# First loads of attention issued in the block before it, scan products moved between levels, gate products paired on opposite array halves

## The chip, the core and the metric

One NeuronCore of a Trainium2 chip runs the whole program. The metric is the device time of one execution in microseconds (us), given as the median of several runs. Names used below: PE is TensorE's matmul, PEld its weight load, DVE is VectorE, ACT is ScalarE, POOL is GpSimd, SP is SyncE, which here only issues transfers. L785 is line 785 of the kernel before.

## What is computed

Two trunk layers run over 128 context tokens and 512 latent tokens, all float32. Layer 0 projects the tokens once (21 blocks of 128 columns) and feeds two head groups: attention with a sink logit, and a bidirectional RWKV-7 time mixer. Layer 1 is a convolution module. Both layers end in an expert retrieval (PEER). The parts of the reference that the change touches are the mixer's decay and learning rate, and its scan:

```python
logw = -jax.nn.softplus(-(w0[idx] + jnp.tanh(wl) @ w2[idx])) - 0.5
decay = jnp.exp(-jnp.exp(logw))
a = jax.nn.sigmoid(a0[idx] + al @ a2[idx])
...
s = (s * w_t[:, :, None, :]
     - jnp.einsum('bhvk,bhk->bhv', s, kh_t)[..., None] * ka_t[:, :, None, :]
     + v_t[..., None] * kt_t[:, :, None, :])
```

and the modulation `jax.nn.silu(cond) @ w + b`, whose weights (mod_w, 48 pieces of 1 MB) are streamed beside other work.

## The kernel before, in words

All TensorE work lies in blocks, one after the other; between two blocks all engines meet at a barrier, and each engine runs its own instructions in the order written.

**The first block** (phase_front, to 267.9 us) normalises the tokens, makes the first modulation rows and projects the 21 column blocks. The projection goes by 42 ticks: in each, TensorE multiplies half a column block (L330, L331), and a side program (`operands`, run by `Side`) puts the mixer's small products between ticks. For step n of 8 (four groups of 128 columns, two directions) `gates(n)` (L335) multiplies the decay weights w2 into bank pair A and the learning-rate weights a2 into bank pair B. Both contract over 64 rows: rows 0 to 63 of the array for direction 0, rows 64 to 127 for direction 1. Each is two matmuls of 320 columns (`mm640`, L205 to L208). ScalarE turns A and B into `ld` and `a` (L482), VectorE builds the scan's operands (`multiply`, L607), and `bonus` (L365, L624) makes a head sum; the last bonus is read by VectorE at L626, four ticks before the end. SP's part of this block only issues loads of column blocks.

**The attention block** (phase_attention, 267.9 to 394.2 us): SP issues the cached keys, the rotation matrix, the cosine and sine table (rope), the mask and others, then modulation steps 0 to 4 into a ring of five 1 MB places (L733 to L738), then small rows. A later step m is issued when step m - 5 has been multiplied (L742 to L744). TensorE turns values and keys, rotates queries and keys (L771), multiplies modulation steps 0 to 3 (L819), and then goes through 20 pairs of heads and query tiles; in each it does the scores of the next pair (L781, L785), two transposes, the weighted values and two modulation steps. 40 steps are streamed in all. When step 38 is done, POOL loads the scan's masks and states.

**The scan block** (phase_scan, 394.2 to about 676 us) goes through 10 chunks of 64 tokens for two directions g. A chunk has five levels of a triangular inverse: `level` multiplies (into M, copied by ScalarE at L1172), `refine` multiplies by it, VectorE merges the result under a mask (L1249), and the next `level` of the same g needs that merge. Then come `solve`, `finish` and the state update (L1279, L1281). Four products of the next chunk (turned_keys, values, first_products, second_products) are prepared meanwhile. `beside` alternates matmuls of its arguments, which use different quadrants of the array. Before the change the order is:

```python
for l in range(LEVELS):
    for g in range(G):
        if l and i + 1 < N:
            beside(level(g, i, l), steps[l - 1](g, i + 1))
        elif l:
            beside(level(g, i, l))
    for g in range(G):
        refine(g, i, l)
    if l == 0:
        for g in range(G):
            beside(weigh_state(g, i))
```

**The trunk** (phase_trunk, from 676 us) does the rest: output projection, layer 1 and both expert retrievals, with 1280 indirect loads. The change doesn't touch it.

Of the kernel before, what the change touches and what calls it, by code (L numbers as in the profile page):

```python
# [173 lines left out]
def mod_lanes(r):  # L174
    return slice(32 * r, 32 * r + 2)
# [38 lines left out]
def phase_front(K, ring, small, normed, dump, u, q1, q2, k1, k2, pc, mixT, low):  # L214
# [17 lines left out]
    with ExitStack() as mem:  # L232
# [25 lines left out]
        with nc.Block() as block:  # L258
            @block.sync
            def _(sp):  # L260
# [35 lines left out]
            def _(pe):  # L296
# [37 lines left out]

                def gates(n):  # L335
                    cols, rows = slice(n // 2 * P, (n // 2 + 1) * P), slice(64 * (n % 2), 64 * (n % 2) + 64)
# [4 lines left out]
                    elif n % 2 == 0 or n == 1:  # L341
                        pe.wait_ge(S["kh_done"], n // 2 + 1)
                    else:
# [21 lines left out]
                def bonus(cc):  # L365
                    if cc == NCC - 1:
                        pe.wait_ge(S["bonus_read"], cc)
                    else:
                        pe.wait_ge(S["a_done"], 2 * cc + 4)
# [8 lines left out]
                def operands():  # L378
# [6 lines left out]
                    for n in range(N):  # L385
                        cc, d = n // 2, n % 2
                        yield step_tick(n)
                        if n + 1 < N:
                            gates(n + 1)
# [35 lines left out]
            def _(act):  # L425
# [56 lines left out]
                def gates(n):  # L482
# [4 lines left out]
                    nc.scalar.activation(ld[:, p, :], ps[:, A, SQ:EQ], ACT.Sigmoid, bias=vcol("ab_w0", 4 * d + cc)).then_inc(S["sig_done"], 1)  # L487
                    act.wait_ge(S["az_done"], n + 1)
# [14 lines left out]
                def operands():  # L503
# [14 lines left out]
                    rates(0)  # L518
                    for n in range(N):
# [142 lines left out]

class ScanParts:
# [5 lines left out]
    def __init__(self, K, u, at):  # L669
# [4 lines left out]
        self.staging = [at(f"levels{n}", [P, self.LM], K.base + 140800 + 8192 * n) for n in range(2)]  # L674
        self.raw = at("raw", [P, G, NCC, CH], K.base + 140800 + 8192 * 2)
# [18 lines left out]
def phase_attention(K, qT, kT, vT, mixT, scan_parts):  # L694
# [3 lines left out]
    with ExitStack() as mem:  # L698
        sb = lambda n, s, d=F32: mem.enter_context(nc.sbuf_tensor("at_" + n, s, d))
        in_x = lambda n, s, at: nc.alloc_sbuf_tensor_at("at_" + n, s, F32, offset=K.x_at + at)  # L700
        ring = sb("ring", [P, MOD_PLACES, 4 * 512])
        mask = sb("mask", [P, 7 * P])
        mod, normg, rope = in_x("mod", [P, MOD_LATER, 512], 0), in_x("normg", [P, 2, 512], 10240), in_x("rope", [P, 2, T_LAT], 14336)
        perm, kctx, vctx, kcT = (in_x(n, [P, P], 18432 + 512 * a) for a, n in enumerate(("perm", "kctx", "vctx", "kcT")))
        kvtok = sb("kvtok", [P, NT + 1, P])
        sink = scan_parts.spare
        s, pT = sb("s", [P, 4, 4 * P]), sb("pT", [P, 2, 4 * P])
        rot = s[:, 2:4, :]
        st = sb("st", [P, 4, 6])
        assert nc.sbuf_base <= K.base + HEADS_AT  # L710
        m_in = [K.sem(f"at_m_in{a}") for a in range(MOD_PLACES)]
# [5 lines left out]
        keys_in, rope_in, rest_in, kv_turned, kv_copied, kv_out = (K.sem("at_" + n) for n in ("keys_in", "rope_in", "rest_in", "kv_turned", "kv_copied", "kv_out"))  # L717
# [6 lines left out]
        with nc.Block() as block:  # L724
            @block.sync
            def _(sp):
                sp.dma_start(kctx[:], io["cache_k"][0, 0].rearrange("t g e -> t (g e)")).then_inc(keys_in, 16)
                sp.dma_start(perm[:], K.const["ropeperm"]).then_inc(keys_in, 16)
# [1756 lines left out]
```

## Time and profile before

| | |
|---|---|
| time, median of 3 runs | 4194.36 us (4193.69 to 4196.37) |
| the profiled execution's own time | 4194.05 us |
| its span in the trace | 4192.3 us |
| first block, to the barrier | 0 to 267.9 us |
| attention block | 267.9 to 394.2 us |
| scan block | 394.2 to about 676 us |
| trunk | the remaining 3516 us |
| busy, share of the span | PE 73%, DVE 65%, ACT 38%, POOL 36% |
| chain that ended last, by engine | DMA 43%, PE 21%, DVE 9%, ACT 5%, issue 4% |

The chain of the page is an average over the whole program, and the trunk, at 84% of the span, fills it. The changed code runs in the first 676 us, so the stages there are read one by one. Times in the trace are counted from the start of the span.

### The profile page before, as it was taken

The page shows a single profiled execution, that of the slowest core. Times are in us where ns is not written, and L with a number is a line of the kernel's source. Part 1 is how long each engine was busy: PE and PEld are TensorE (multiplying, and loading weights), DVE is VectorE, ACT ScalarE, POOL GpSimd, SP SyncE. Part 2 cuts the span into 40 slices and gives each one's busy share as a digit, 9 for nine tenths or more (in the row PEclk, how much of TensorE's full clock was granted, in tenths as well). Part 3 has the DMA queues.
Part 4 walks back from the last instruction along what each step waited for, and adds up shares of the span by engine and source line. Part 5 has one row for each costly group of instructions (what it writes and reads, how often), then busy time and mean ns, then how long its engine had stood idle before and what let it go on. Part 6 is the DMA issues. An engine that isn't in the chain of part 4 may idle for free.

```text
span 4192.3 us, 67991 instructions
## 1 busy us (share of the span) xinstructions
PE 3054.5 (73%) x25020; PEld 1460.5 (35%) x25020; DVE 2745.0 (65%) x6901; ACT 1596.6 (38%) x4953; POOL 1489.7 (36%) x1307
## 2 busy tenths in 40 slices
PE   8988878887875555588866768887685666666555
PEld 5645776433331111134421434442241231132111
DVE  2646445776666676667876566786756787756764
ACT  3524322343332332345533334553333463322332
POOL 0000000443444444434533444454434454443433
PEclk9999999989997777799987988998798898888877
DMA  4147002999999999999999999999999999999998
GB/s 170 41 184 288 7 4 113 409 420 420 419 412 419 412 419 421 417 412 402 420 396 363 419 420 419 416 420 411 395 419 421 421 419 417 415 419 417 413 421 334
DMA packets 228426, 1507.71 MB, mean 360 GB/s; under 512 B 31086, under 2 KB 32073, under 8 KB 57601
## 3 DMA queue, kind: packets, MB, share of 16 engines
q0 software_dynamic: 185216, 1343.99, 77.7%
q1 hardware_dynamic: 42440, 159.26, 9.7%
q8 instruction: 202, 3.31, 0.3%
q14 instruction: 126, 1.03, 0.1%
q10 hardware_dynamic: 442, 0.12, 0.0%
HBM read 1500.17 MB, written 3.10 MB: 359 GB/s over the span
## 4 chain that ended last, share of the span: by engine, by line
DMA 43%; PE 21%; DVE 9%; ACT 5%; issue 4%; POOL 2%; SPq 0%; PEldq 0%; ACTq 0%; POOLq 0%; DVEq 0%
DMA t_ring<-in_peer_uv,t_eidx 41%; PE t_ps L2419 10%; DVE t_ring L1747 6%; PE t_ps L2297 2%; POOL t_ring L1609 2%; PE t_ps L2316 1%; ACT t_dg L1938 1%; ACT t_wgt L1932 1%; DMA t_wq<-in_cv_w_pw 1%; PE t_ps L2345 1%; PE t_ps L2161 1%; PE t_ps L2253 1%; PE t_ps L2375 1%; ACT t_wgt L1927 1%; PE t_ps L2257 1%
## 5 line engine op out<-in xcount | busy, mean ns | idle before, releaser
L1609 POOL DMA_INDIRECT t_ring<-in_peer_uv,t_eidx x1280 | 1477.0, 1154 | 2302.2 <-PE t_ps L2422 1799.0
L2419 PE MATMUL t_ps<-t_ring,t_dg 64*64 64x512 f32 x2560 | 1556.2, 739 | 991.4 <-ACT t_dg L1938 934.4
L1747 DVE SCALAR_TENSOR_TENSOR t_ring<-t_ring,t_hring 128x1024 f32<-128x1024 f32 x1024 | 1255.8, 1227 | 772.9 <-DMA t_ring<-in_peer_uv,t_eidx 723.3
L2422 PE MATMUL t_ps<-t_ring,t_dg 64*64 64x512 f32 x2560 | 1572.7, 746 | 0.0
L2421 PE MATMUL t_ps<-t_ring,t_dg 64*64 64x512 f32 x2560 | 1572.5, 746 | 0.0
L2420 PE MATMUL t_ps<-t_ring,t_dg 64*64 64x512 f32 x2560 | 1572.2, 746 | 0.0
L2419 PEld LDWEIGHTS t_ps<-t_ring,t_dg 64*64 64x64 f32 x2560 | 344.3, 155 | 1981.2 <-issue 1954.8
L1927 ACT ACTIVATE t_wgt<-t_dots 128x2 f32<-128x2 f32 x640 | 130.3, 204 | 1916.3 <-DVE t_ring L1747 1874.9
L1938 ACT ACTIVATE t_dg<-t_eye,t_wgt 128x64 f32<-128x64 f32 x1280 | 376.0, 340 | 1.3 <-ACT t_wgt L1932 1.1
L2422 PEld LDWEIGHTS t_ps<-t_ring,t_dg 64*64 64x64 f32 x2560 | 345.0, 156 | 0.0
L2421 PEld LDWEIGHTS t_ps<-t_ring,t_dg 64*64 64x64 f32 x2560 | 344.9, 156 | 0.0
L2420 PEld LDWEIGHTS t_ps<-t_ring,t_dg 64*64 64x64 f32 x2560 | 344.8, 156 | 0.0
L1932 ACT ACTIVATE t_wgt<-t_wgt,t_gate 128x1 f32<-128x1 f32 x1280 | 307.3, 287 | 28.5 <-DVE t_gate L1722 2.8
L1747 DVE SCALAR_TENSOR_TENSOR t_ring<-t_ring,t_h_latent 128x1024 f32<-128x1024 f32 x128 | 157.2, 1228 | 116.1 <-DMA t_ring<-in_peer_uv,t_eidx 102.8
L1747 DVE SCALAR_TENSOR_TENSOR t_ring<-t_ring,t_h_context 128x1024 f32<-128x1024 f32 x128 | 156.9, 1226 | 97.6 <-DMA t_ring<-in_peer_uv,t_eidx 94.7
L2316 PE MATMUL t_ps<-t_glu,t_diag 128*128 128x256 f32 (+1 forms) x930 | 188.8, 356 | 0.0
L2316 PEld LDWEIGHTS t_ps<-t_glu,t_diag 128*128 128x128 f32 x930 | 153.5, 194 | 68.0 <-ACT t_diag L1994 39.6
L1927 ACT ACT_TABLE_LOAD x113 | 145.0, 1283 | 17.1 <-DVE t_ring L1747 15.2
L2375 PE MATMUL t_ps<-t_pair,t_wq 128*128 128x256 f32 (+1 forms) x768 | 151.3, 351 | 0.0
L1994 ACT ACTIVATE t_diag<-ident,vec 128x128 f32<-128x128 f32 x465 | 143.3, 387 | 0.9 <-PE t_ps L2316 0.6
L2375 PEld LDWEIGHTS t_ps<-t_pair,t_wq 128*128 128x128 f32 x768 | 129.1, 198 | 15.2 <-issue 3.2
L684 POOL DMA_DIRECT2D ev_u<-const_scanmask x1 | 0.6, 557 | 367.9 <-PE at_mps L819 367.9
(385 smaller groups left out, 4499.2 us busy)
## 6 DMA issues: line engine op xcount, KB each, us to landing
at_ring<-in_mod_w SPq DMA_DIRECT2D x40, 1024.0 KB, 10.9
t_wq<-in_peer_w_q SPq DMA_DIRECT2D x62, 512.0 KB
t_ring<-in_peer_uv,t_eidx POOLq DMA_INDIRECT x1280
t_wg<-in_cv_w_pw SPq DMA_DIRECT2D x32, 512.0 KB
t_wq<-in_cv_w_pw SPq DMA_DIRECT2D x24, 512.0 KB
fr_wring<-in_ab_w_in SPq DMA_DIRECT2D x21, 512.0 KB, 3.5
ev_mod_ring<-in_mod_w SPq DMA_DIRECT2D x8, 1024.0 KB, 18.5
t_wg<-in_peer_w_q SPq DMA_DIRECT2D x16, 512.0 KB
```

The lines of the kernel that those rows point to most:

```text
L1609: pool.indirect_dma_start(ring[:, place[n], :], None, table, bass.IndirectOffsetOnAxis(ap=eidx[:, s % 2, r:r + 1], axis=0)).then_inc(row_i ...
L1747: V.scalar_tensor_tensor(ring[:, place[n], 0:D], ring[:, place[n], 0:D], 1.0, h_of(j), ALU.mult, ALU.mult, accum_out=dots[:, j % 2, r:r + ...
L1927: nc.scalar.activation(wgt[:, r:r + 2], dots[:, j % 2, r:r + 2], ACT.Gelu).then_inc(S["gelu_done"], 1)
L1932: nc.scalar.activation(wgt[:, r + b:r + b + 1], wgt[:, r + b:r + b + 1], ACT.Copy, scale=gate[:, j % 2, r + b:r + b + 1]).then_inc(S["wgt_ ...
L1938: nc.scalar.activation(dg[:, n % DIAGS, :], eye[:], ACT.Copy, scale=wgt[:, r + b:r + b + 1]).then_inc(S["diag_set"], 1)
L1994: nc.scalar.activation(diag[:, n % BATCH, :], ident[:], ACT.Copy, scale=K.vec[:, col:col + 1]).then_inc(S["diag_ready"], 1)
L2316: nc.tensor.matmul(tiles_of(banks[:, 4 + b % 2, :], p), diag[:, n % BATCH, :], windows(p, b, w), start=(w == 0), stop=(w == CONVW - 1)).th ...
L2375: last = nc.tensor.matmul(tiles_of(banks[:, 6 + b % 2, :], p), wq[:, n % 2, k, :], both[:, k, 0:E, :], start=(k == 0), stop=(k == KD - 1))
L2419: nc.tensor.matmul(straight[low], diagonal[low], row[low, 0:512], **ends)
L2420: nc.tensor.matmul(straight[high], diagonal[high], row[high, 0:512], **ends)
L2421: nc.tensor.matmul(crossed[high], diagonal[low], row[low, 512:D], **ends)
L2422: nc.tensor.matmul(crossed[low], diagonal[high], row[high, 512:D], **ends).then_inc(S["used"], 1)
```

## The change

Three things are done, and one follows from them.

1. **Gate products.** `gates(n)` now makes the decay product of step n and the learning-rate product of step n - 1, in four alternating matmuls (first 320 columns of both, then last 320 of both). Step n and step n - 1 have opposite directions, so the two products lie on opposite 64-row halves of the array. Step 0 has the decay product alone, and a new `gates(8)` has the last learning-rate product alone. ScalarE's `gates` is split, and `learning(n)` follows `gates(n + 1)`.
2. **First loads of attention.** After VectorE's last bonus read, SP issues keys, rotation matrix, rope table and modulation steps 0 to 3 in the first block. For that the five ring places are moved (two lie in the x area, two over the front's small weights, the fifth where the transposed tokens lie until the end of the projection, so step 4 is still issued in the attention block).
3. **Scan order.** turned_keys is put beside weigh_state instead of beside level 1. For levels 2 to 4 the product of g = 0 runs alone before `level(0, i, l)`, and that of g = 1 stays beside `level(1, i, l)`.
4. Tiles of the scan and of attention move in memory; VectorE waits for the mask copies before it clears the state, which now lies where the masks were staged.

```diff
@@ phase_front, sync @@
+                sp.wait_ge(S["bonus_read"], NCC)
+                attention_parts.load_ahead(sp, K)
@@ phase_front, tensor @@
                 def gates(n):
+                    halves = ((SQ, 512, 0, SPLIT), (512, EQ, SPLIT, T))
...
-                    mm640(nc, ps, A, w2[rows, cols], u[rows, 12, :]).then_inc(S["z_done"], 1)
-                    if n in (4, 6):
+                    if n >= 4 and n % 2 == 0:
                         pe.wait_ge(S["bonus_read"], n // 2 - 1)
-                    elif n:
-                        pe.wait_ge(S["a_done"], n)
-                    mm640(nc, ps, B, a2[rows, cols], u[rows, 13, :]).then_inc(S["az_done"], 1)
+                    elif n >= 2:
+                        pe.wait_ge(S["a_done"], n - 1)
+                    for lo, hi, first, last in halves:
+                        if n < N:
+                            cols, rows = gate_of(n)
+                            z = nc.tensor.matmul(ps[:, A, lo:hi], w2[rows, cols], u[rows, 12, first:last], start=True, stop=True)
...
+                        if n:
+                            cols, rows = gate_of(n - 1)
+                            az = nc.tensor.matmul(ps[:, B, lo:hi], a2[rows, cols], u[rows, 13, first:last], start=True, stop=True)
...
@@ phase_front, scalar @@
-                            rates(n + 1)
+                        learning(n)
+                        rates(n)
                         exponents(n)
@@ AttentionParts (new) @@
+    def load_ahead(self, sp, K):
+        sp.dma_start(self.kctx[:], ...).then_inc(self.keys_in, 16)
+        sp.dma_start(self.perm[:], ...).then_inc(self.keys_in, 16)
+        sp.dma_start(self.rope[:], ...).then_inc(self.rope_in, 16)
+        for m in range(MOD_EARLY):
+            self.load_step(sp, K, m)
@@ phase_attention, sync @@
-                for m in range(MOD_PLACES):
-                    load_step(m)
+                for m in range(MOD_EARLY, MOD_PLACES):
+                    parts.load_step(sp, K, m)
@@ phase_scan, tensor @@
+                    ahead = i + 1 < N
+                    for g in range(G):
+                        refine(g, i, 0)
+                    for g in range(G):
+                        if ahead:
+                            beside(weigh_state(g, i), turned_keys(g, i + 1))
+                        else:
+                            beside(weigh_state(g, i))
+                    for l in range(1, LEVELS):
+                        if ahead and l > 1:
+                            beside(steps[l - 1](0, i + 1))
+                        beside(level(0, i, l))
+                        if ahead and l > 1:
+                            beside(level(1, i, l), steps[l - 1](1, i + 1))
+                        else:
+                            beside(level(1, i, l))
                         for g in range(G):
                             refine(g, i, l)
```

## Rows read from the trace of the kernel before

**Rows 1.** the page: the span; TensorE's granted clock in 40 slices

```profile
span 4192.3 us, 67991 instructions
...
PEclk9999999989997777799987988998798898888877
```

**Rows 2.** stages: length, busy PE, PEld, DVE, ACT, POOL; PEclk, DMA, GB/s

```profile
60.00:267.00 207.00, 205.08 (x733) 136.65 (x731) 103.86 (x152) 88.62 (x125) 0.00 (x0) 0.98 0.13 44
267.00:394.00 127.00, 101.86 (x841) 43.49 (x841) 86.31 (x281) 52.94 (x169) 5.19 (x9) 0.93 0.89 355
394.00:676.00 282.00, 234.73 (x9344) 218.61 (x9344) 129.64 (x265) 83.32 (x242) 0.00 (x0) 0.99 0.05 15
676.00:4192.00 3516.00, 2472.98 (x13888) 1036.49 (x13888) 2409.57 (x6168) 1353.37 (x4384) 1476.97 (x1280) 0.86 0.99 408
```

**Rows 3.** timeline, TensorE: first and last matmul of one step's gates

```profile
157.50 0.80 PE L207 MATMUL fr_ps<-ev_u,fr_w 64*128 64x320 f32 x2
...
159.22 0.70 PE L208 MATMUL fr_ps<-ev_u,fr_a 64*128 64x320 f32 x2
```

**Rows 4.** the line view of L785: durations, then matmuls in a moment

```profile
L785 PE MATMUL at_ps_s<-ev_u x4: 482/484/485, 330.9 to 331.2; 64*128 64x384 f32 x4
...
331.19:331.23 0.04, 0.04 (x4) 0.00 (x0) 1.00 0.51 205
```

**Rows 5.** timeline, around the last bonus product (start us, length, engine)

```profile
239.06 0.88 DVE L649 SCALAR_TENSOR_TENSOR ev_kt<-ev_ktsum,fr_rkh,ev_u 128x640 f32<-128x640 f32 x1
...
252.74 0.70 PE L207 MATMUL fr_ps<-ev_kt,fr_hsum 128*128 128x320 f32 x2
...
254.01 0.82 DVE L626 TENSOR_TENSOR ev_u<-fr_ps,ev_u 128x640 f32<-128x640 f32 x1 [14.07 <-PE fr_ps L208]
```

**Rows 6.** timeline, first loads and rotations of the attention block

```profile
267.90 0.33 SPq L727 DMA_DIRECT2D at_kctx<-in_cache_k  x1
...
273.19 0.69 DVE L850 TENSOR_TENSOR at_s<-at_ps_s,at_rope 128x512 f32<-128x512 f32 x1 [18.36 <-DMA at_rope<-const_rope]
...
278.67 0.50 PEld L771 LDWEIGHTS at_ps_s<-ev_u,at_perm 128*128 128x128 f32 x2 [1.53 <-DVEq L853]
...
282.62 28.15 SPq L734 DMA_DIRECT2D at_ring<-in_mod_w  x12
...
284.93 1.04 PE L819 MATMUL at_mps<-at_ring,csil 128*2 128x512 f32 x8 [1.03 <-DMA at_ring<-in_mod_w]
```

**Rows 7.** stretches of the attention block, columns as in rows 2

```profile
270.00:275.00 5.00, 2.45 (x6) 1.04 (x7) 1.66 (x3) 0.54 (x2) 0.00 (x0) 1.00 0.82 250
275.00:279.50 4.50, 3.59 (x5) 1.01 (x4) 4.21 (x8) 0.00 (x0) 0.00 (x0) 0.65 0.96 406
...
300.00:330.00 30.00, 25.29 (x228) 9.70 (x220) 21.89 (x74) 11.50 (x42) 0.00 (x0) 1.00 1.01 419
```

**Rows 8.** the modulation ring: its issues, who waited for its transfers

```profile
at_ring<-in_mod_w SPq DMA_DIRECT2D x40, 1024.0 KB, 10.9
...
  PEld at_mps L819: 22.9, 17
```

**Rows 9.** eight chunks of the scan, and the slowest, columns as in rows 2

```profile
433.85:654.20 220.35, 180.58 (x7458) 167.47 (x7447) 101.45 (x209) 66.56 (x195) 0.00 (x0) 1.00 0.03 6
570.82:601.49 30.67, 22.68 (x946) 20.96 (x950) 12.63 (x27) 8.24 (x25) 0.00 (x0) 1.00 0.02 4
```

**Rows 10.** TensorE's waits in the scan: us, times, longest

```profile
PE sc_ps L1014 <- issue: 30.7, 40, 1.8
PE sc_ps L1014 <- DVE ev_u L1249: 10.5, 24, 0.6
```

**Rows 11.** the scan between two idle times; the instruction queue's packets

```profile
552.13 0.27 PE L1014 MATMUL sc_ps<-ev_u 64*64 64x64 f32 x2 [0.73 <-issue]
...
552.13:556.03 3.90, 2.66 (x127) 2.52 (x128) 1.00 0.02 4
...
q8 instruction: 74, 1.21, 1.7%
```

More of the change, by code:

```diff
@@ L211, with phase_front @@
 ORDER = [D_AIN // P + j for j in (12, 13, 4, 5, 6, 7, 0, 14, 8, 1, 9, 2, 10, 3, 11)] + [0, 1, 2, 4, 5, 3]
-def phase_front(K, ring, small, normed, dump, u, q1, q2, k1, k2, pc, mixT, low):
+def phase_front(K, ring, small, normed, dump, u, q1, q2, k1, k2, pc, mixT, low, attention_parts):
     nc, io, x, ident = K.nc, K.io, K.x, K.ident
@@ L333, in project, with gate_of @@
                         last.then_inc(S["block_done"], 1)
+                def gate_of(n):
+                    return slice(n // 2 * P, (n // 2 + 1) * P), slice(64 * (n % 2), 64 * (n % 2) + 64)
                 def gates(n):
[L336 removed]
+                    halves = ((SQ, 512, 0, SPLIT), (512, EQ, SPLIT, T))
                     if n == 0:
@@ L487, in gates, with learning @@
                     nc.scalar.activation(ld[:, p, :], ps[:, A, SQ:EQ], ACT.Sigmoid, bias=vcol("ab_w0", 4 * d + cc)).then_inc(S["sig_done"], 1)
+                def learning(n):
+                    cc, d, p = n // 2, n % 2, n % 2
                     act.wait_ge(S["az_done"], n + 1)
@@ L673, in __init__ @@
         self.spare = u[:, 14, 0:HEADS]
-        self.staging = [at(f"levels{n}", [P, self.LM], K.base + 140800 + 8192 * n) for n in range(2)]
-        self.raw = at("raw", [P, G, NCC, CH], K.base + 140800 + 8192 * 2)
+        self.staging = [at(f"levels{n}", [P, self.LM], K.base + 177664 + 3072 * n) for n in range(2)]
+        self.raw = at("raw", [P, G, NCC, CH], K.base + 175616)
         K.heads = at("heads", [P, 2, P], K.base + HEADS_AT)
@@ L699, in phase_attention @@
         sb = lambda n, s, d=F32: mem.enter_context(nc.sbuf_tensor("at_" + n, s, d))
[L700 to L705, printed above, removed]
-        sink = scan_parts.spare
-        s, pT = sb("s", [P, 4, 4 * P]), sb("pT", [P, 2, 4 * P])
+        places, rope, perm, kctx = parts.places, parts.rope, parts.perm, parts.kctx
+        m_in, keys_in, rope_in = parts.m_in, parts.keys_in, parts.rope_in
+        sink = scan_parts.spare
+        sb("place4", [P, 4 * 512])
+        normg, mod = sb("normg", [P, 2, 512]), sb("mod", [P, MOD_LATER, 512])
+        mask, kvtok = sb("mask", [P, 7 * P]), sb("kvtok", [P, NT + 1, P])
+        vctx, kcT = sb("vctx", [P, P]), sb("kcT", [P, P])
+        pT, st = sb("pT", [P, 2, 4 * P]), sb("st", [P, 4, 6])
+        assert nc.sbuf_base <= K.base + 175616
+        sb("between", [P, (K.base + 192000 - nc.sbuf_base) // 4])
+        s = sb("s", [P, 4, 4 * P])
         rot = s[:, 2:4, :]
-        st = sb("st", [P, 4, 6])
-        assert nc.sbuf_base <= K.base + HEADS_AT
-        m_in = [K.sem(f"at_m_in{a}") for a in range(MOD_PLACES)]
+        assert nc.sbuf_base <= K.base + 200192
         mps = mem.enter_context(nc.psum_tensor("at_mps", [P, 2, 512], F32))
@@ L818, in modulation @@
                     for r in range(4):
-                        last = nc.tensor.matmul(mps[mod_lanes(r), g % 2, :], K.csil[:, k, :], ring[:, m % MOD_PLACES, r * 512:(r + 1) * 512],
+                        last = nc.tensor.matmul(mps[mod_lanes(r), g % 2, :], K.csil[:, k, :], places[m % MOD_PLACES][:, r * 512:(r + 1) * 512],
                                                 start=(k == 0), stop=(k == KD - 1))
@@ L1130, in _ @@
                 for i in range(N):
-                    for l in range(LEVELS):
-                        for g in range(G):
-                            if l and i + 1 < N:
-                                beside(level(g, i, l), steps[l - 1](g, i + 1))
-                            elif l:
-                                beside(level(g, i, l))
+                    ahead = i + 1 < N
[14 more added lines that the diff above has]
+                            beside(level(1, i, l))
                         for g in range(G):
                             refine(g, i, l)
-                        if l == 0:
-                            for g in range(G):
-                                beside(weigh_state(g, i))
                     for g in range(G):
```

53 lines of the change are left out of this document (34 added, 19 removed).

## The prediction

> **What bounds the kernel now.** I read the page first, then stretches by stage, then timelines and waits. The page gives a span of 4192.3 us [rows 1]. The stage view [rows 2] splits it, and each stage has its own limit. From 60 to 267 us PE is busy for 205.1 of 207 us: the projection is limited by TensorE, and whatever leaves its queue leaves the time. From 267 to 394 us the transfers are at 355 GB/s, in the middle at 419 GB/s with a share of 1.01 [rows 7]: attention is limited by the stream of modulation weights, and weight loads of L819 wait 22.9 us for them [rows 8]. From 394 to 676 us no engine is full: PE 234.7 of 282 us. The rest is two kinds of waits: 10.5 us for VectorE's masked merge (24 times), and 30.7 us, 40 times, of "issue", in which TensorE waited for nothing that the profile shows [rows 10]. The trunk keeps the DMA engines at 0.99 for 3516 us; nothing in it is touched and it starts at a barrier, so it should move as a whole by what the first three stages give.
>
> The sum is made against the profiled execution's own 4194.05 us, which is 1.75 us more than its span. The median of the runs is 4194.36, 0.3 us higher.
>
> **Part 1, gate products.** In a step four matmuls of 64 rows and 320 columns start at 157.50 to 159.22 us, in even steps: the last begins 1.72 us after the first, so one takes about 0.54 us after the extra 0.1 us of the first [rows 3]. Four are 2.15 us a step, eight steps 17.2 us, all in TensorE's full queue. Do opposite halves overlap? The scores of the two head groups lie on opposite halves in separate banks, as the new pairs will: at 331.2 us four of their records, of 0.48 us each, run at once, and all four start between 330.9 and 331.2 [rows 4]. Two after two would need twice that. So an interleaved pair should take the time of one. New sum: step 0 alone 1.07, seven paired visits 7 x 1.07, the last learning-rate product 1.07, in all 9.7 us. **Gain 7.5 us.** Bounds: no overlap 0, full overlap 7.5; I take 7.5, since the row is the same form.
>
> What moves with it: `a` of step n comes one gate visit later, still in the same step, and VectorE makes the running sums of step n + 1 before it wants it. The tight place is the end. Before, VectorE finished the last bonus operand at 239.06 + 0.88 us, and TensorE took it up at 252.74 - 0.13, a margin of over 12 us [rows 5]. The last learning rate now comes at tick 35, one tick ahead of the last output gate: about 238.7 us by the old clock, ready for VectorE near 241, where the old `multiply` of step 7 began at 233.2. The bonus operand then ends near 239.9 + 7.8 = 247.7, and about 5 us of margin are left. If they were gone, TensorE would stand there and the loads behind it too. ScalarE has the same instructions in another order, and costs nothing while TensorE is full.
>
> **Part 2, loads ahead.** VectorE reads the last bonus at 254.01 + 0.82 us [rows 5]; the block ends 13 us later, when SP issues the keys at 267.90 [rows 6]. Both move with part 1. SP has nothing queued behind its new wait except the barrier, where TensorE arrives 12 us later. The seven issues take about 0.45 us each (3.2 us) and leave the attention block's SP queue; mask, sink, values and step 4 go 3 us sooner. Nothing else moves data there, so 4.85 MB (four steps of 1.05, rope 0.52, two of 0.07) land in about 11.6 us at 419 GB/s, near the barrier.
>
> Times now are counted with the barrier at its old place. Rope was waited for until 273.19 us [rows 6]; now VectorE starts when the first rotation is made, near 269.7. The chain is 3.5 us earlier, its last rotation at 278.67 - 3.5 = 275.2. Step 0 follows, near 275.8. PE's granted clock is 0.65 from 275 to 279.5 us, so partly at the lower level of 1.2 GHz [rows 7], after rotations with idle time between them, which the new order keeps. A step takes 0.95 us at the full clock [rows 6] and twice that at the lower. So step 0 is done near 277.7, step 5 is issued, and its data moves from about 279.5. Before that the ring has a dry spell: only mask, values and step 4 are asked for. This is the price of moving four loads and not the fifth.
>
> Compare bytes at 279.5 us. New: 4.85 ahead + 0.46 + 0.07 + 1.05 and small rows = 6.6 MB. Old: 0.2 + 5 x 0.250 + 4.5 x 0.406 = 3.3 MB [rows 7]. Later both stream at 0.419 MB/us with the same ring, so the new one is 3.3 / 0.419 = **8 us ahead**, and SP's tail, POOL's loads and the barrier with it. Bounds: if pairs, not transfers, set the pace, only the rope's 3.5 us; if the dry spell costs nothing, four steps of 2.5 us, 10 us. The narrow early pairs have slack to catch up with the stream, so I take 8.
>
> **Part 3, scan order.** A product of four head pairs takes about 0.47 us, a merged one of eight about 1.05. Putting turned_keys beside weigh_state saves about 0.94 us of a chunk, of which 0.2 comes back as a wait for the copy of M. In levels 2 to 4 a lone product of 0.5 to 0.9 us fills a wait of 10.5 / 24 = 0.44 us and makes level 0's half shorter: some 0.2 us each. By this walk a chunk gains 1.3 us, nine chunks 12 us.
>
> But the issue idles have a pattern. From one at 552.13 to the next at 556.03 us are 127 matmuls and 128 weight loads, 3.90 us [rows 11]; I found 22 more such neighbours, 126 to 128 matmuls apart, 3.4 to 5.0 us, mean 3.84. Over the scan the instruction queue moved 1.21 MB in 74 packets [rows 11], 16 KB each, one per 3.8 us. So TensorE waits for its own instructions, one packet per 128 matmuls. Eight chunks took 220.35 us with 7458 matmuls: 27.5 us a chunk, 7.3 packets, 3.78 us a packet [rows 9]. That is already the interval between starved neighbours. The reordering removes no instruction, so what it saves turns into a longer issue idle. Bounds: the full 12 us, or a loss if every packet took 3.84 us: 0.06 x 65 = 4 us. I take **2 us**, near the fetch-limited end, as most chunks are there.
> The Trainium skill, "Runtime: NRT & Kernel Launch", section "Instruction fetch mechanics", says that crossing a 16 KiB boundary costs one DMA tail-bump and is mostly hidden. By that rule the walk's 12 us would come. The trace disagrees so far, with 0.77 us of idle per starved boundary.
>
> The wait for the mask copies costs nothing: VectorE's queue holds both copies ahead of it, and TensorE is at its first products then.
>
> **Sum:** 7.5 + 8 + 2 = 17.5 us. 4194.05 - 17.5 + 0.3 = 4176.9; I say 4177.
>
> **Rivals.**
> - *Fetch is not the limit.* Against: the even spacing. For: 74 packets stand against 40 issue idles, so close to half of the boundaries show none. Then 12 in place of 2: 4167. Chance 0.15.
> - *Attention turns to the pairs' pace.* For: in the wide pairs PE is nearly full. Then 3.5 in place of 8: 4181. Chance 0.14.
> - *The pairing doesn't happen*: the array takes both halves in turn, 0 in place of 7.5: 4184. Against: rows 4. Chance 0.06.
> - *Slower.* Instruction fetch gets worse where TensorE is denser and waits for nothing else. The slowest chunk took 30.67 us [rows 9], 3.1 more than the mean. If all nine became like it, 28 us more: 4194.4 - 15.5 + 28 = 4207. A packet interval of 4.0 us over nine chunks (0.22 x 66 = 14.5 us) eats the other gains, and one of 4.2 gives the 28. Chance 0.04.
> - *Most of it is given back*, by the margin at the end of the front and by starved packets together: 4188 to 4194. Chance 0.1.
>
> **Numbers.** The forecast has 0.51. 0.2% is 8.4 us, about what a measurement of this kernel can tell from no change, so faster means below 4186. Forecast, the first two rivals and most of the third lie there: 0.84. The fifth and a piece of the third give 0.12 for no change, the slower rival 0.04. The range reaches from just below the first rival, 4163, to 4188, which leaves out the slower rival and part of the fifth.
>
> **What would show it.** Right: the block's barrier 7.5 us earlier, seven gate visits with all four matmuls within some 1.3 us; SP's loads near 247 us; rope no longer waited for; a stretch of low transfer rate between the barrier and step 5; last ring issue some 15 us earlier; scan chunks of about 27.3 us with fewer waits on L1249 and more issue idle. Wrong: chunks near 26 us without issue idles, or above 28; weight loads of a pair starting one after the other; no wait of L819 for transfers in the early pairs.

## The result

The changed kernel takes 4170.92 us (median of 5 runs, 4169.54 to 4176.78), the kernel before 4194.36 beside it: ratio 0.9947, 95% interval 0.9936 to 0.9957. Its profiled execution took 4169.54 us. The page of the changed kernel:

```profile
span 4167.8 us, 67998 instructions
...
PE 3026.0 (73%) x25020; PEld 1449.8 (35%) x25020; DVE 2744.5 (66%) x6901; ACT 1600.3 (38%) x4955; POOL 1518.4 (36%) x1307
...
PEclk9999999999997877799977979998897897888787
```

Its stages, with their borders at the barriers and at the first matmul of the trunk; columns as in [rows 2]:

```profile
60.00:259.49 199.49, 195.72 (x730) 130.19 (x728) 103.75 (x152) 90.48 (x126) 0.00 (x0) 0.99 0.20 68
259.49:375.43 115.94, 96.95 (x841) 44.32 (x842) 86.29 (x281) 52.20 (x168) 5.18 (x9) 0.96 0.87 349
375.43:662.00 286.57, 233.10 (x9344) 217.39 (x9344) 129.39 (x265) 83.14 (x242) 0.00 (x0) 0.99 0.05 14
662.00:4167.80 3505.80, 2459.99 (x13888) 1031.76 (x13888) 2409.22 (x6167) 1355.31 (x4384) 1505.68 (x1280) 0.86 1.00 409
```

To set beside them, the same borders of before are 267.90, 394.20 and 677.92 us. So the first block is 8.4 us shorter, attention 10.4 us shorter (115.9 for 126.3), the scan **2.9 us longer** (286.6 for 283.7) and the trunk, which nobody touched, 8.6 us shorter (3505.8 for 3514.4). In all 24.5 us of span, 15.9 of them in the three stages that the change touches.

**Gates.** The timeline of TensorE over one step (start us, length, engine), to set beside [rows 3]:

```profile
151.94 0.53 PE L357 MATMUL fr_ps<-ev_u,fr_w 64*128 64x320 f32 x1
151.95 0.53 PE L362 MATMUL fr_ps<-ev_u,fr_a 64*128 64x320 f32 x1
...
152.86 0.43 PE L357 MATMUL fr_ps<-ev_u,fr_w 64*128 64x320 f32 x1
152.86 0.43 PE L362 MATMUL fr_ps<-ev_u,fr_a 64*128 64x320 f32 x1
153.22 0.81 PE L332 MATMUL fr_ps<-fr_hT,fr_wring 128*128 128x320 f32 x2
```

Each decay product (L357) and the learning-rate product of the other half (L362) start together. From the first to the projection's next matmul are 1.28 us; before, 157.50 to 159.84, it was 2.34.

**End of the front and loads ahead.** The timeline around the last bonus, and of the attention block's first operations:

```profile
238.35 0.89 DVE L666 SCALAR_TENSOR_TENSOR ev_kt<-ev_ktsum,fr_rkh,ev_u 128x640 f32<-128x640 f32 x1
...
244.31 0.70 PE L207 MATMUL fr_ps<-ev_kt,fr_hsum 128*128 128x320 f32 x2
...
245.59 0.82 DVE L643 TENSOR_TENSOR ev_u<-fr_ps,ev_u 128x640 f32<-128x640 f32 x1 [6.36 <-PE fr_ps L208]
246.44 0.33 SPq L695 DMA_DIRECT2D ev_kctx<-in_cache_k  x1
...
247.76 1.90 SPq L692 DMA_DIRECT2D ev_mod_place<-in_mod_w  x4
...
261.45 0.69 DVE L884 TENSOR_TENSOR at_s<-at_ps_s,ev_rope 128x512 f32<-128x512 f32 x1 [15.03 <-PE at_ps_s L805]
...
267.98 3.61 PE L853 MATMUL at_mps<-ev_mod_place,csil 128*2 128x512 f32 x32
...
269.08 2.90 SPq L692 DMA_DIRECT2D ev_mod_place<-in_mod_w  x4
```

VectorE finished the last bonus operand at 239.24 us (238.35 + 0.89) and TensorE took it up at 244.31 - 0.13, so the margin was 4.9 us and held. Rope is no longer waited for: VectorE's first rotation comes 2.0 us after the barrier and not 5.3, and what it waited for is PE. Step 5 is issued 9.6 us after the barrier. Transfers between, and the clock (columns as in [rows 2]):

```profile
264.00:266.00 2.00, 1.11 (x2) 0.30 (x2) 1.85 (x4) 0.00 (x0) 0.00 (x0) 1.00 1.03 402
266.00:268.00 2.00, 1.09 (x7) 0.32 (x9) 1.85 (x4) 0.00 (x0) 0.00 (x0) 1.00 0.31 86
268.00:270.00 2.00, 2.00 (x21) 0.50 (x24) 1.85 (x4) 0.00 (x0) 0.00 (x0) 1.00 0.13 33
```

This is the dry spell. The last issue of the ring is at 352.63 us, 18.7 us earlier than before (371.33).

**Scan.** The eight chunks that answer to [rows 9]:

```profile
416.77:638.18 221.41, 178.87 (x7455) 166.69 (x7447) 100.91 (x209) 66.37 (x195) 0.00 (x0) 1.00 0.03 6
```

TensorE's waits over these eight chunks, as in [rows 10]:

```profile
PE sc_ps L1050 <- issue: 36.6, 41, 2.0
PE sc_ps L1088 <- issue: 3.2, 5, 1.0
```

And the packets of the instruction queue in them (packets, MB, share):

```profile
q8 instruction: 59, 0.97, 1.9%
```

The 8.9 us for the masked merge that the same eight chunks of before had are gone, and the issue idles grew from 27.8 to 39.8 us. The eight chunks take 221.4 us for 220.4, with 59 packets in both kernels.

### The profile page after: what moved, and what is told of

The parts are those of the page before. It is cut to its first block, busy times and chain, and to the rows that moved or that the text cites. A ratio compares the mean times of both kernels' runs of the same rounds, so it can differ in the third digit from the quotient of the medians.

```text
span 4167.8 us, 67998 instructions
## 1 busy us (share of the span) xinstructions
PE 3026.0 (73%) x25020; PEld 1449.8 (35%) x25020; DVE 2744.5 (66%) x6901; ACT 1600.3 (38%) x4955; POOL 1518.4 (36%) x1307
## 4 chain that ended last, share of the span: by engine, by line
DMA 46%; PE 19%; DVE 8%; ACT 5%; issue 3%; POOL 3%; SPq 0%; POOLq 0%; PEldq 0%; ACTq 0%; DVEq 0%
DMA t_ring<-in_peer_uv,t_eidx 44%; PE t_ps L2463 9%; DVE t_ring L1791 5%; POOL t_ring L1653 3%; PE t_ps L2341 2%; PE t_ps L2360 2%; ACT t_dg L1982 1%; DMA t_wq<-in_cv_w_pw 1%; ACT t_wgt L1976 1%; PE t_ps L2389 1%; PE t_ps L2419 1%; ACT t_wgt L1971 1%; PE t_ps L2205 1%; PE t_ps L2464 1%; ACT L1971 0%
## 5 line engine op out<-in xcount | busy, mean ns | idle before, releaser
L1653 POOL DMA_INDIRECT t_ring<-in_peer_uv,t_eidx x1280 | 1505.7, 1176 | 2266.7 <-PE t_ps L2466 1751.9
L1982 ACT ACTIVATE t_dg<-t_eye,t_wgt 128x64 f32<-128x64 f32 x1280 | 376.6, 340 | 1.0 <-ACT t_wgt L1976 0.2
```

The lines of the kernel that those rows point to most:

```text
L1653: pool.indirect_dma_start(ring[:, place[n], :], None, table, bass.IndirectOffsetOnAxis(ap=eidx[:, s % 2, r:r + 1], axis=0)).then_inc(row_i ...
L1982: nc.scalar.activation(dg[:, n % DIAGS, :], eye[:], ACT.Copy, scale=wgt[:, r + b:r + b + 1]).then_inc(S["diag_set"], 1)
```

## Experiments

In the table "barrier" is the end of the first block, "scan" goes from its first matmul to the trunk's first, "eight chunks" between the last state updates of the first and the ninth chunk, "trunk" from there to the end of the last instruction with a tile, all of one profile each; the medians are of all runs, and one in brackets is a single run. The kernel before was timed again beside each group: 4191.01 us beside gates alone, loads alone, scan order alone and gates and loads; 4193.41 beside again, same half, delay and five ahead; 4187.81 beside six ahead, fewer instructions and the two halves. These three medians of one kernel differ by 5.6 us.

| kernel | barrier | attention | scan | eight chunks | trunk starts | trunk | median | ratio, 95% |
|---|---|---|---|---|---|---|---|---|
| before | 267.9 | 126.3 | 283.7 | 220.4 | 677.9 | 3511.3 | 4194.36 | |
| changed | 259.5 | 115.9 | 286.6 | 221.4 | 662.0 | 3502.7 | 4170.92 | 0.9936 to 0.9957 |
| changed, again | 259.5 | 115.8 | 287.5 | 221.0 | 662.8 | 3501.7 | 4169.20 | 0.9927 to 0.9954 |
| gates alone | 260.1 | 126.5 | 284.8 | 221.5 | 671.4 | 3503.7 | 4179.56 | 0.9962 to 0.9983 |
| loads alone | 267.9 | 117.6 | 284.8 | 220.2 | 670.2 | 3505.2 | 4179.73 | 0.9958 to 0.9983 |
| scan order alone | 267.9 | 126.3 | 285.5 | 219.8 | 679.8 | 3509.5 | 4190.99 | 0.9991 to 1.0009 |
| gates and loads | 260.5 | 115.5 | 283.4 | 219.6 | 659.3 | 3504.5 | 4170.46 | 0.9941 to 0.9968 |
| same half | 268.1 | 115.6 | 285.8 | 221.3 | 669.6 | 3504.9 | (4179.32) | |
| delay | 260.2 | 115.5 | 301.7 | 218.8 | 677.4 | 3504.8 | 4192.00 | 0.9990 to 1.0009 |
| five ahead | 260.1 | 116.5 | 282.9 | 218.7 | 659.5 | 3502.7 | 4169.31 | 0.9930 to 0.9957 |
| six ahead | 259.3 | 114.2 | 282.0 | 217.6 | 655.4 | 3509.0 | 4168.28 | 0.9936 to 0.9963 |
| fewer instructions | 259.8 | 115.7 | 275.4 | 211.0 | 650.9 | 3500.8 | (4156.54) | |
| half, new order | 259.3 | 118.0 | 315.0 | 246.7 | 692.3 | 3506.0 | (4203.19) | |
| half, old order | 259.2 | 118.2 | 338.3 | 268.9 | 715.7 | 3508.2 | (4228.73) | |

**Gates alone.** The kernel before with the change of `gates`, `bonus` and `rates` only:

```diff
-                    mm640(nc, ps, A, w2[rows, cols], u[rows, 12, :]).then_inc(S["z_done"], 1)
...
+                    for lo, hi, first, last in halves:
...
+                            z = nc.tensor.matmul(ps[:, A, lo:hi], w2[rows, cols], u[rows, 12, first:last], start=True, stop=True)
...
+                            az = nc.tensor.matmul(ps[:, B, lo:hi], a2[rows, cols], u[rows, 13, first:last], start=True, stop=True)
```

> The kernel before with the gate products alone changed. My theory: four matmuls of opposite halves take the time of two, so the first block's barrier comes 7.5 to 8.5 us earlier (267.9 to about 259.8 us) and attention and scan keep their lengths, 126.3 and 283.7 us; in all about 4186. Rival A, the pairing is worth nothing and the earlier barrier of the changed kernel came from less time at the lower clock: barrier within 3 us of 267.9. Of the trunk: if its 8.6 us shorter time in the changed kernel was caused by the new attention or scan, it stays near 3514 us here; if it comes from where the trunk falls in time or varies from run to run, it may be anywhere from 3503 to 3516.

The barrier came at 260.1, 7.8 us earlier, and attention and scan kept their lengths within 1.1 us. The theory stands, the rival falls. The median is 4179.56 beside 4191.01, so 11.5 us lower where 8 were expected: here too the trunk is short (3503.7), with the attention and the scan of before, so its shorter time needs neither of their changes.

**Same half.** One line of the changed kernel:

```diff
-                            cols, rows = gate_of(n - 1)
+                            cols, rows = gate_of(n - 1)[0], gate_of(n)[1]
```

> The changed kernel in which the learning-rate product of a visit takes the rows of the decay product beside it, so both stand on the same half of the array (the learning rates come out with the other direction's weights and are wrong). Same matmuls in the same order. Theory of the opposite halves: each of seven visits takes four times 0.54 us and not two, so the barrier of the first block comes 7 x 1.07 = 7.5 us later, at 267.0. Rival, the interleaving or the order gives the gain and not the halves: barrier at 259.5.

The timeline of a visit shows the two kinds taking turns, 0.54 us a product (two records of the trace, 0.27 us each), and the barrier's first issue comes where it was before:

```profile
155.78 0.80 PE L357 MATMUL fr_ps<-ev_u,fr_w 64*128 64x320 f32 x2
...
156.42 0.70 PE L362 MATMUL fr_ps<-ev_u,fr_a 64*128 64x320 f32 x2
...
156.96 0.70 PE L357 MATMUL fr_ps<-ev_u,fr_w 64*128 64x320 f32 x2
...
157.49 0.70 PE L362 MATMUL fr_ps<-ev_u,fr_a 64*128 64x320 f32 x2
...
268.13 0.33 SPq L767 DMA_DIRECT2D at_mask<-const_amask  x1
```

Same matmuls in the same order, 8.6 us later than in the changed kernel: the opposite halves are the whole gain. It is 1.1 us more than expected, because the second visit took 3.5 us in this profile: the granted clock was 0.50 from 124.4 to 131.2 us. The other six took 2.35 us each.

**Loads alone.** The kernel before with `AttentionParts`, its places and these lines:

```diff
+                sp.wait_ge(S["bonus_read"], NCC)
+                attention_parts.load_ahead(sp, K)
```

> The kernel before with the loads ahead alone (and the new places in memory). My theory: first block unchanged (barrier near 267.9), attention 116 to 118 us in place of 126.3, scan unchanged at about 283.7; in all about 4185. Rival: the gain in attention needed the denser first block of the paired gates, which left the clock at its higher level for step 0; then attention takes 118 to 120 us. As with the first kernel the trunk tells whether its 8.6 us belong to a part of the change.

Attention took 117.6 us, within the theory's numbers, but 1.7 us longer than in the changed kernel. Here TensorE's clock fell in the rotations, and steps 0 and 1 ran at the lower level; the four steps took 4.66 us, where the changed kernel's took 3.61:

```profile
272.00:274.00 2.00, 1.09 (x3) 0.30 (x2) 1.85 (x4) 0.00 (x0) 0.00 (x0) 1.00 0.67 260
274.00:276.00 2.00, 1.09 (x3) 0.30 (x2) 1.85 (x5) 0.00 (x0) 0.00 (x0) 0.93 0.79 294
276.00:278.00 2.00, 2.00 (x10) 0.25 (x12) 1.85 (x4) 0.00 (x0) 0.00 (x0) 0.50 0.17 44
278.00:280.00 2.00, 2.00 (x17) 0.34 (x12) 1.85 (x4) 0.00 (x0) 0.00 (x0) 0.72 0.14 30
```

Step 5 was issued 11.0 us after the barrier in place of 9.6. In the changed kernel the same rotations and steps have a granted clock of 1.00 (the windows above). So the loads are worth 8.7 us in this profile, and 10.4 with the clock still high.

The rival says that the paired gates kept the clock up. Two other kernels speak against it. *Half of the products* is the changed kernel up to the scan, paired gates and all, and in both of its profiles the clock fell in the rotations just so, with 118.0 and 118.2 us of attention:

```profile
267.00:269.00 2.00, 2.00 (x6) 0.15 (x9) 1.85 (x4) 0.00 (x0) 0.00 (x0) 0.57 0.24 77
269.00:271.00 2.00, 2.00 (x16) 0.39 (x12) 1.85 (x4) 0.00 (x0) 0.00 (x0) 0.57 0.05 14
```

*Same half*, whose gates gain nothing, kept the clock, issued step 5 at 9.6 us after its barrier and took 115.6 us:

```profile
276.00:278.00 2.00, 2.00 (x18) 0.40 (x20) 1.85 (x4) 0.00 (x0) 0.00 (x0) 1.00 0.28 81
```

So the clock in the rotations can go either way with the same code up to there, and it is worth some 2 us of attention. What decides it isn't shown. The median of loads alone is 4179.73 beside 4191.01, 11.3 us lower where 9 were expected.

**Scan order alone**, and **gates and loads** with the old order, were each the before or the changed kernel with this part in the other form:

```diff
-                            if l and i + 1 < N:
-                                beside(level(g, i, l), steps[l - 1](g, i + 1))
...
+                            beside(weigh_state(g, i), turned_keys(g, i + 1))
...
+                        if ahead and l > 1:
+                            beside(steps[l - 1](0, i + 1))
```

> The kernel before with the scan's order alone changed. Theory of the instruction fetch: the waits for the merge vanish and the time stays, since not one instruction is removed: scan 283.7 to 287 us against 283.7, time 0 to 3 us above before, packets of the instruction queue 3.76 to 3.80 us apart. Rival, the scan of the changed kernel is held back by something the other parts brought (the moved staging places, the memory): then the scan gets shorter here, by up to 12 us.

> The changed kernel with the scan's old order, that is the gates and the loads alone. Theory: as fast as the changed kernel or up to 3 us faster, so 4168 to 4172; scan 283.7 us in place of 286.6. Rival, the new order helps the time as a whole (by the state in which it leaves the trunk): 4176 to 4180, with a trunk of 3514 us.

The order alone lengthened the scan by 1.8 us and changed the median by nothing; without it the changed kernel's scan is 3.2 us shorter. Over all profiles the old order takes 282.0 to 284.8 us (six, mean 283.6), the new one 285.5 to 287.5 (four, mean 286.4). These two ranges don't touch. But with the delay kernel as a fifth of the new order they do, up to the last state update of the ninth chunk: 257.8 to 261.0 us in the old order, 259.2 to 263.4 in the new one. By the means 1.0 us more lies ahead of the first chunk's last state update (41.2 for 40.1 us) and 0.8 in the eight chunks (220.5 for 219.6). So the new order probably costs 1 to 3 us; the profiles of one order differ by as much among themselves, and the medians don't show it. Eight chunks of the scan order alone, then TensorE's waits in them:

```profile
435.66:655.45 219.79, 179.00 (x7458) 167.02 (x7448) 100.83 (x208) 66.34 (x194) 0.00 (x0) 1.00 0.03 6
```

```profile
PE sc_ps L1014 <- issue: 37.2, 45, 2.0
PE sc_ps L1014 <- DVE ev_u L1254: 1.2, 7, 0.2
```

The queue moved 59 packets in them. Again the waits went and issue idle took their place.

**Fewer instructions.** The changed kernel, `heads` of the chunk's output with one half of each pair after the first chunk:

```diff
-                            for e in range(2):
+                            for e in range(both):
...
-                    yield from heads(region(g, 5), None, (at(state(i), g), chunk(q2, g, i)), (v, at(BD[:, i % 2, :, 1], g)), (at(U, g), at(ET[:, i % 2], g)))
+                    yield from heads(region(g, 5), None, (at(state(i), g), chunk(q2, g, i)), (v, at(BD[:, i % 2, :, 1], g)), (at(U, g), at(ET[:, i % 2], g)), both=2 if i == 0 else 1)
```

> The changed kernel; from the second chunk on, the second half of each pair of products of the chunk's output (24 of some 932 matmuls of a chunk, and their 24 weight loads) is left out, so half of the heads have no output of the scan there. A pair on opposite halves runs side by side, so TensorE saves no time by it. Theory of the fetch: 48 instructions less are 0.19 of a 16 KB packet, at 3.78 us 0.7 us a chunk and 5.7 us over eight; scan 281 to 282 us against 287, packets still 3.75 to 3.80 us apart. Rival, the engine's own work or the chain of merges sets the chunk: scan 286 to 287.5.

Its eight chunks, then the packets in them:

```profile
417.82:628.77 210.95, 177.90 (x7088) 167.11 (x7083) 99.18 (x208) 66.42 (x194) 0.00 (x0) 1.00 0.03 6
```

```profile
q8 instruction: 56, 0.92, 1.8%
```

**Half of the products**, in the new and in the old order: the same `both` in nearly all products of the scan. What is left of each pair lies on one half of the array's rows, rows 0 to 63 for most products and rows 64 to 127 for some (`refine`, `solve`).

> The changed kernel; from the second chunk on nearly all products of the scan are made for the first half of each pair alone (its other half of the heads is wrong), so a chunk has about half its instructions and each pair's time is that of its first matmul. Theory of the fetch: 3.7 packets a chunk need 14 us and are no limit; a chunk falls from 27.6 us to what the walk of products and copies gives, 22 to 24.5 us, the issue idles are gone, and waits for merges and copies are back. Rival, packets don't matter: 27 us as now, or, if the two halves did not overlap after all, far below 20.

> The same half of the products with the scan's old order (and gates and loads as changed). Theory: without the fetch limit the new order is worth what the walk gave it, so a chunk takes 1.3 us more here than in the new order, 10 us over eight chunks. Rival, the walk itself was wrong and the new order is worth nothing even then: within 0.3 us a chunk.

The eight chunks and 200 us out of their middle, in the new and then in the old order:

```profile
414.26:661.00 246.74, 245.31 (x3755) 239.34 (x3751) 102.94 (x208) 66.47 (x194) 0.00 (x0) 0.53 0.02 3
...
461.00:661.00 200.00, 199.33 (x2927) 195.19 (x2927) 79.94 (x162) 51.87 (x151) 0.00 (x0) 0.50 0.01 2
```

```profile
415.46:684.37 268.91, 262.03 (x3755) 252.48 (x3751) 103.13 (x209) 66.99 (x195) 0.00 (x0) 0.54 0.01 3
...
461.00:661.00 200.00, 197.13 (x2660) 190.26 (x2657) 72.34 (x145) 48.23 (x139) 0.00 (x0) 0.50 0.01 2
```

Their packets in the eight chunks, new order:

```profile
q8 instruction: 30, 0.49, 0.8%
```

and 31 in the old one. Half of the work took **longer**, 30.8 and 33.6 us a chunk. None of the numbers that I gave came, since the clock fell: in the new order the granted clock is 0.50 from 435 us to the end of the scan, with TensorE busy 99% of the time; in the old one it was 1.00 for a while around 450 us and is 0.50 from 461 us on. But two things can be read. A packet lasts 8.2 and 8.7 us here, and in the new order the list of matmul waits is empty from 440 us on: with half of the packets the fetch is no limit. And where it is none, the new order is the faster one: in the same 200 us at the same clock it makes 2927 matmuls and the old one 2660, 10% more. In the last six of the eight chunks, all at 0.50, that is 31.6 us a chunk for 35.0. The direction is the walk's, from one profile of each kernel. What the order is worth with few instructions at the full clock was not measured.

**Five and six steps ahead**, both with the old scan order. The fifth step goes to a place that is dead after the last bonus; the sixth is asked for at the barrier, without a wait, into the place that step 4 had. From the kernel of six ahead:

```diff
+        self.first4 = at("mod_place4_first", [P, 4 * 512], K.base)
...
-        for m in range(MOD_EARLY):
+        for m in range(MOD_EARLY + 1):
...
-                for m in range(MOD_EARLY, MOD_PLACES):
-                    parts.load_step(sp, K, m)
+                parts.load_step(sp, K, MOD_EARLY + 1)
```

> Gates and loads of the changed kernel, the scan's old order, and the fifth step of weights loaded ahead as well, into the place of en and kt, which nothing reads after the last bonus. Theory: the dry spell of the ring (0.1 to 0.3 of the transfer rate for 5 us) gets longer by what the fifth step used of it, but the stream is one step of 1.05 MB ahead: last issue of the ring 2 to 2.5 us earlier than 353.19, scan starts near 373.7, about 2 us below the kernel of gates and loads: 4168. Rival, the pairs' pace is the limit by then and nothing is gained: scan starts at 376.

> Gates and loads of the changed kernel, old scan order, step 4 loaded ahead into the place of en and kt, and step 5 asked for at the barrier without a wait into the place that step 4 had, so that there is something to move in the dry spell. Theory: the fifth step alone gave nothing because it landed in the dry spell anyway; a sixth fills it, and the stream from then on is one step, 1.05 MB / 0.42 = 2.5 us, ahead: scan starts at 373 to 374 in place of 376, in all 4167. Rival, TensorE's pairs set the pace by now (its waits for transfers fell from 12.9 to 6.1 us with the fifth step ahead and the scan began no sooner): 376, and 4169 to 4170 as now.

Five ahead missed: the scan began at 376.6, and the last issue came 0.6 us later. As I read it, it could not have gained, because in the kernel of gates and loads step 4 had landed in the dry spell anyway; the next thing that moves, step 5, was issued at 269.72 and 270.05 us, 9.6 us after the barrier in both. That attention is 1.0 us longer says little: in that profile the granted clock was 0.50 for 10.2 us of the block's first 40, in that of gates and loads for 3.4. Six ahead began the scan at 373.5 us, in the range expected, with 261 GB/s over five us where the changed kernel has 118 (265 to 270 us):

```profile
264.00:269.00 5.00, 3.40 (x16) 0.92 (x20) 4.56 (x8) 0.00 (x0) 0.00 (x0) 1.00 0.69 261
```

That is 1.3 us of attention, half of the 2.5 us expected; 1.2 us of the earlier start are the barrier's. In the median it doesn't show (4168.28 beside a before of 4187.81, the changed kernel's 4169.20 beside 4193.41), so no version here is measurably faster than the changed kernel, though this one's trunk starts 6.6 us earlier.

**The trunk.** Two kernels were to show where its 8.6 us come from: the changed kernel once more, and the changed kernel with copies on ScalarE at the end of the scan:

```diff
+                for n in range(18):
+                    if n:
+                        act.wait_ge(held, n)
+                    nc.scalar.copy(XX[:, 1], XX[:, 0]).then_inc(held, 1)
```

> The changed kernel once more, among more runs of before. The first three stages differ by 16 us between the two profiles (8.4 + 10.4 - 2.9), the medians by 23.4. Theory: what is over comes from the trunk's own variation, so the medians differ by 16 to 21 us here. Rival, the trunk is really shorter in the changed kernel: 22 to 25 us again, and a trunk (first matmul to the end) near 3503 us.

> The changed kernel with some 20 us of copies on ScalarE between scan and trunk, so that the trunk starts near 680 us, where it starts in the kernel before. Theory that the trunk's length depends on when it starts: 3508 to 3512 us as in before and in the kernel with the scan's order alone. Rival, it varies from run to run whatever comes ahead: it may as well be 3502 to 3506 as in the four other profiles.

For the changed kernel the medians differ by 24.2 us, where the first three stages give 15.1: the rival's numbers came. For the delay the rival's number came too (3504.8 us of trunk). But the other kernels don't repeat it: what their medians gain beyond their earlier start of the trunk is 5.0 (gates alone), 3.6 (loads alone), 2.0 (gates and loads), 5.7 (five ahead) and -3.0 us (six ahead). The trunk in the table lies between 3500.8 and 3511.3 us, and the long one was the profile of before. Set side by side from the trunk's start, VectorE's operations stay within 3.3 us of before up to 2199 us (in before); then before and the scan order alone lose some 4 to 8 us to the others (2.5 to six ahead) within some 80 us, most of it in the first 35. This is the place in before, and in the changed kernel's second profile:

```profile
2203.00:2208.00 5.00, 5.00 (x24) 1.91 (x24) 2.46 (x6) 0.00 (x0) 1.83 (x2) 1.00 0.98 364
2208.00:2213.00 5.00, 1.49 (x13) 0.54 (x6) 1.45 (x5) 3.96 (x8) 1.88 (x2) 0.87 1.01 423
2213.00:2218.00 5.00, 5.00 (x7) 1.97 (x6) 1.53 (x10) 0.00 (x0) 0.00 (x0) 0.50 1.01 421
2218.00:2223.00 5.00, 5.00 (x23) 1.62 (x23) 0.00 (x0) 0.00 (x0) 1.88 (x2) 0.95 0.29 66
```

```profile
2187.00:2192.00 5.00, 3.85 (x21) 1.08 (x19) 2.22 (x9) 0.94 (x5) 2.60 (x2) 1.00 1.01 409
2192.00:2197.00 5.00, 4.87 (x20) 1.95 (x24) 2.28 (x10) 3.02 (x5) 0.94 (x1) 1.00 1.03 429
2197.00:2202.00 5.00, 4.70 (x20) 1.67 (x16) 0.53 (x1) 0.00 (x0) 1.88 (x2) 1.00 1.02 423
2202.00:2207.00 5.00, 3.53 (x32) 0.96 (x24) 5.00 (x13) 1.18 (x5) 2.98 (x3) 1.00 0.93 354
```

The timeline of before has behind its stop:

```profile
2212.43 6.71 PE L2345 MATMUL t_ps<-t_wq,t_pair 128*128 128x512 f32 x8 [3.51 <-DMA t_wq<-in_cv_w_pw]
```

There TensorE waits 3.51 us, to 2212.43, for a transfer of convolution weights. Its clock falls to 0.50, and its next eight matmuls take 6.71 us where they take 3.70 in the other. SP, which may issue the next piece only when they are done, waits 5.2 us for them, and five us later the transfers are down to 66 GB/s. In the other the wait at this place is 1.28 us, the clock stays at 1.00 and the transfers have no such gap. The scan order alone waited 3.52 us here and six ahead 2.02, and in both the clock fell for 3.4 us; in the kernels that went the quick way the wait is at most 1.5 us.

Why the transfer comes late in some is not settled. The profile of the delay kernel, whose trunk starts at 677.4 us, goes the quick way (3504.8), so a late start alone does not force it. But that profile is the fastest of its 10 runs (4186.94 to 4195.79), and its median is 22.8 us above the changed kernel's for a start that is 14.6 us later. Median less start of the trunk is 3509.9 to 3516.4 us where the trunk starts at 677 to 680 (before by its four medians, scan order alone, delay), and 3506.4 to 3512.9 for the others, which overlaps. So up to 8 us may hang on the time at which the trunk starts, or it is scatter; this stays open.

## Why the prediction was right, and where it was not

Forecast 4177 (4163 to 4188), measured 4170.92: faster, as the forecast had it, and inside the range. The sum was 17.5 us, the three stages gave 15.9 in the first pair of profiles, and the medians 23.4. That sum and stages lie only 1.6 us apart is luck: two terms came out 0.9 and 2.4 us larger, above their upper bounds of 7.5 and 10, and the third 4.9 us smaller.

- **Part 1, 7.5 us.** The mechanism is shown by the same-half run. Size 8.4 in the profile, 7.8 in the gates alone; over all profiles with paired gates the barrier lies between 259.2 and 260.5 us. The 0.6 between the two lie ahead of the gates, whose first product came at 115.21 us in the changed kernel for 115.85 in before; from there to the barrier both are shorter than before by 7.7 to 7.8. My 0.54 us a matmul left out the change-over, which nearly cancels: a whole visit was 2.34 us, not 2.15, and is 1.28, so 1.06 are saved where I had 1.07. What no sum of mine had is the clock: the second visit of before took 3.47 us, with a granted clock of 0.50 from 126.2 us.
- **The margin at the last bonus**, put at about 5 us, was 4.9. It held.
- **Part 2, 8 us.** Mechanism right (rope not waited for, dry spell, step 5 at 9.8 us after the barrier and in fact 9.6), size 10.4. The step that failed is "step 0 at the lower clock": in the changed kernel steps 0 to 3 ran at the full clock, all four in 3.61 us, and freed four places in a row from 269.08 on. In three profiles the clock was low there, as I had taken it, and attention took 117.6, 118.0 and 118.2 us, a gain of 8.1 to 8.7, near the 8 of the sum.
- **Part 3, 2 us of gain**: the sign was wrong, 2.9 us of loss in the profile, 1.8 in the run of this part alone, inside the bounds of -4 to 12. The reason given, that the packets of instructions set the pace and savings turn into issue idle, is what the runs show: 59 packets and 217.6 to 221.5 us in every kernel with all instructions, 56 and 211.0 with fewer. What failed is the 2 us that I took for chunks that are not starved: together the eight gave nothing. Why the denser order seems to lose some 1 to 3 us and not just break even stays open.
The Trainium skill, "Runtime: NRT & Kernel Launch", section "Instruction fetch mechanics", has the crossing of a boundary as mostly hidden. These runs disagree for this scan: 3.69 to 3.75 us a packet over the eight chunks, in either order.
- **"The trunk moves as a whole"** was wrong by 8.6 us in the profiles and some 7 to 9 in the medians of the changed kernel. With the three stages alone the result would have been 4194.4 - 15.9 = 4178.5, near the forecast of 4177; the other 7.5 us are the trunk's, and how much of them the change causes isn't shown.
- **The rivals.** *Fetch is not the limit* (4167) came near in time and is refuted in its reason. *The pairing doesn't happen* fell with the same-half kernel. *Attention turns to the pairs' pace* (3.5 in place of 8) fell with the 10.4 us: the weight loads of L853 still wait 10.7 us for transfers. *Slower* needed packets of 4.0 us; they stayed at 3.75. *Most of it is given back* didn't come either.

## What to carry to other kernels

Where many small matmuls stand in a row, count instructions: idle times marked "issue" that return every 128 matmuls are the sign. Here a better order then earned nothing, and leaving out three packets of 16 KB earned 10.5 us, even of products that run beside another. A load moved ahead helps only as far as it is the next that the ring would have waited for, so look at what was going to land in the idle time anyway. Before a difference of 2 us is given to a change, compare the granted clock of both profiles at that place: here it went either way with the same code. And a long stage limited by transfers can move by as much as the change is worth; compare stage by stage before a part is given the credit.

## What the hardware did that I had not expected

- Half of the products cost more time than all of them: 246.7 and 268.9 us for eight chunks that take 221.4 with all. In the new order TensorE was busy for 0.99 of the time with the product of one half of each pair, and its granted clock stayed at 0.50 for over 200 us; with both products of each pair it is 1.00 through the eight chunks.
- With the loads ahead, the clock fell in the rotations of attention in three profiles and not in the changed kernel's, and two of the three have the changed kernel's code up to the scan. It cost some 2 us.
- One wait of TensorE for a transfer, 3.5 us in the trunk, stands at the head of a loss of some 4 to 8 us: behind it the clock was 0.50, and the transfers, which wait for its products, fell to 66 GB/s.
